# A convolution mixer's products moved to two-bank PSUM form, and VectorE's weight splits put behind short chains at other places

## What is computed

```python
def _swiglu(x, w_gate_up, w_down):
    a, b = jnp.split(x @ w_gate_up, 2, axis=-1)
    return (jax.nn.silu(a) * b) @ w_down

def _short_conv(x, w_in, conv_w, w_out):
    b_gate, c_gate, u = jnp.split(x @ w_in, 3, axis=-1)
    v = c_gate * u
    conv = lax.conv_general_dilated(
        v, conv_w[:, None, :], window_strides=(1,), padding=[(CONV_WIDTH - 1, 0)],
        dimension_numbers=("NWC", "WIO", "NWC"), feature_group_count=D_MODEL)
    return (b_gate * conv) @ w_out
```

## Time and profile before

| | before |
|---|---|
| median of 3 runs | 1669.12 us (1668.87 to 1671.68) |
| the profiled execution, its own time | 1668.95 us |
| span of its trace | 1667.1 us |
| TensorE busy | 1645.2 us (99% of the span) |
| weight loads of TensorE | 1420.7 us (85%) |
| VectorE busy | 1017.7 us (61%) |
| ScalarE busy | 793.6 us (48%) |
| GpSimd busy | 69.0 us (4%) |
| mean granted clock of TensorE | 0.996 |
| moved by DMA | 294.82 MB, mean 177 GB/s |

### The profile page before, as it was taken

The page is one execution under the profiler, slowest core; times in us unless marked ns, Lnnn a source line. Parts: engine busy times, 40 slices in busy tenths (PEclk is TensorE's granted clock), DMA queues, the critical chain, the costliest instruction groups (busy, mean ns, idle before and its releaser), DMA issues.

```text
span 1667.1 us, 22598 instructions
## 1 busy us (share of the span) xinstructions
PE 1645.2 (99%) x9497; PEld 1420.7 (85%) x9497; DVE 1017.7 (61%) x1076; ACT 793.6 (48%) x958; POOL 69.0 (4%) x73
## 2 busy tenths in 40 slices
PE   9999999999999999999999999999999999999999
PEld 7998888889888887888899888888888887688887
DVE  6676655575565557556576556565664477765555
ACT  5334544455454445444543444455443355744443
POOL 0122000000000001000000000000100002000000
PEclk9999999999999999999999999999999999999999
DMA  8534567554356565565565555647545462055562
GB/s 286 163 127 135 189 190 217 200 193 164 125 180 197 177 203 164 200 211 171 189 215 177 173 188 171 209 166 223 196 157 192 171 198 96 1 197 184 176 207 95
DMA packets 221110, 294.82 MB, mean 177 GB/s; under 512 B 7516, under 2 KB 184880, under 8 KB 221010
## 3 DMA queue, kind: packets, MB, share of 16 engines
q1 hardware_dynamic: 215546, 284.40, 51.4%
q10 hardware_dynamic: 5464, 9.00, 2.1%
HBM read 290.75 MB, written 1.57 MB: 175 GB/s over the span
## 4 chain that ended last, share of the span: by engine, by line
PE 86%; DVE 7%; ACT 3%; DMA 2%; issue 1%; POOL 1%; SPq 0%; DVEq 0%; POOLq 0%; ACTq 0%
PE ps L1929 24%; PE ps L2066 18%; PE ps L1931 13%; PE ps L1917 3%; PE ps L1920 3%; PE ps L1918 3%; PE ps L1946 3%; PE ps L1952 3%; PE ps L1947 3%; DVE wlo L1238 2%; PE ps L1996 2%; PE ps L1997 1%; PE ps L1998 1%; PE ps L2182 1%; ACT whi L672 1%
## 5 line engine op out<-in xcount | busy, mean ns | idle before, releaser
L1238 DVE TENSOR_TENSOR wlo<-raw,whi 128x2048 fp32r<-128x2048 f32 (+2 forms) x281 | 603.8, 2166 | 306.8 <-ACT whi L672 305.6
L672 ACT ACTIVATE whi<-raw 128x2048 fp32r<-128x2048 f32 (+1 forms) x265 | 498.4, 1900 | 81.5 <-PE ps L1920 17.9
L1929 PE MATMUL ps<-x_both,whi 128*128 128x512 f32 x1920 | 480.3, 392 | 0.0
L1929 PEld LDWEIGHTS ps<-x_both,whi 128*128 128x128 f32 x1920 | 348.6, 189 | 64.7
L1931 PEld LDWEIGHTS ps<-x_both,wlo 128*128 128x128 f32 x1920 | 261.9, 190 | 18.7
L1931 PE MATMUL ps<-x_both,wlo 128*128 128x256 f32 x1920 | 267.7, 282 | 0.0
L2066 PE MATMUL ps<-whi,hhi 128*128 128x512 f32 x480 | 188.9, 393 | 0.0
L2066 PE MATMUL ps<-wlo,hhi 128*128 128x512 f32 x480 | 188.1, 392 | 0.0
L2066 PE MATMUL ps<-whi,hlo 128*128 128x512 f32 x480 | 187.4, 390 | 0.0
L1917 PE MATMUL ps<-x_both,whi 128*128 128x256 f32 x512 | 127.7, 287 | 0.0
L768 ACT ACTIVATE hid<-ps 128x512 f32<-128x512 f32 x54 | 32.2, 597 | 196.6 <-PE ps L1931 196.5
(11 more groups left out here) (255 smaller groups left out, 1704.6 us busy)
## 6 DMA issues: line engine op xcount, KB each, us to landing
raw<-in_ffn_w_gate_up SPq DMA_DIRECT2D x80, 1024.0 KB, 5.2
raw<-in_ffn_w SPq DMA_DIRECT2D x62, 1024.0 KB, 5.3
raw<-in_ffn_w_down SPq DMA_DIRECT2D x44, 1024.0 KB, 4.8
raw<-in_hgrn_w_in SPq DMA_DIRECT2D x16, 1024.0 KB, 5.5
raw<-in_moba_w_in SPq DMA_DIRECT2D x12, 1024.0 KB, 5.1
raw<-in_conv_w_in SPq DMA_DIRECT2D x10, 1024.0 KB, 5.2
raw<-in_ffn_w_gate_up SPq DMA_DIRECT2D x16, 512.0 KB, 5.0
raw<-in_kv_w SPq DMA_DIRECT2D x6, 1024.0 KB, 5.1
```

The source lines that it names most:

```text
L672: act.activation(whi[s % WRING][:, 0:width], raw[n % RING][:, 0:width], ACT.Copy).then_inc(split_hi, 1)
L1238: ins = dve.tensor_tensor(wlo[s % WRING][:, part], raw[n % RING][:, part], whi[s % WRING][:, part].bitcast(F32), ALU.subtract)
L1929: pe.matmul(ps[:, bank + n, :], hi[:, k, tile], x_both[:, k], start=k == 0, stop=k == KT - 1, skip_group_check=True)
```

## The change

It has four parts.

1. `conv`: `c`, `u` and `b` of all rounds go by `across_pair`, in banks 0-1, 4-5 and 2-3. ScalarE copies the upper part of each (`c_low`, `u_low`, `b_low`), VectorE adds. The first quarter of `cy` is split during round 2 already, into `hhi` and `hlo`. The idle products are gone; the output product begins with the quarter that is ready (`ks=(0, 1)` of both chunks), and goes on with the rest. VectorE's `split(out, 2)` moves behind the last splits of `cy`.
2. `moba`: `scale_probs(3)` stands ahead of `split(out, 2)` on VectorE.
3. Ends of stages: in mixers VectorE's `split(first, 1)` moves behind the two adds of t=0, and ScalarE's squares of t=1 behind `x_high` of t=0. In FFNs the first half of `split(first, 1)` moves behind `normalise` of t=0; in `ffn1` the second half, and the add that follows it, also move behind the second norm's scaling.
4. `ffn4`, rounds 5 to 8: VectorE's `split(d)` moves behind `multiply` and `low_part`.

```diff
@@ scalar: out_product
-                squares(after, 1, 0)
                 x_high(after, 0)
-                squares(after, 1, 1)
+                for half in range(2):
+                    squares(after, 1, half)
                 x_high(after, 1)
@@ scalar: conv
+                def c_low(i):
+                    act.wait_ge(chunk_used, chunks.number[name, "c", i] + 1)
+                    act.wait_ge(gated, i + 1)
+                    act.activation(cgate[:], ps[:, 0:2, S:2 * S], ACT.Copy).then_inc(gate_kept, 1)
+                def u_low(i):
...
+                    act.activation(hid[:], ps[:, 4:6, S:2 * S], ACT.Copy).then_inc(u_low_kept, 1)
+                def b_low(i):
...
+                    act.activation(silu[:], ps[:, 2:4, S:2 * S], ACT.Copy).then_inc(b_low_kept, 1)
...
                 split(name, "u", 1)
+                b_low(0)
                 split(name, "b", 1)
                 for i in range(1, 4):
...
+                    split(*((name, "c", i + 1) if i < 3 else (name, "out", 0)))
+                    c_low(i)
+                    split(*((name, "u", i + 1) if i < 3 else (name, "out", 1)))
+                    u_low(i)
+                    if i == 2:
+                        act.wait_ge(conv_round_done, 1)
+                        act.activation(hhi[:], cy[:, 0:2, :], ACT.Copy).then_inc(yhi_ready, 1)
+                    split(*((name, "b", i + 1) if i < 3 else (name, "out", 2)))
+                    b_low(i)
+                for p in range(1, 4):
@@ vector: out_product
-                for n in range(2):
-                    split(after, "first", n)
+                split(after, "first", 0)
                 for half in range(2):
                     dve.wait_ge(tile_summed, 2 * MIXERS.index(name) + half + 1)
                     add(0, half)
+                split(after, "first", 1)
                 normalise(after, 0)
@@ vector: ffn, in the loop
+                    beside = name == "ffn4" and i in COMPRESS
+                    if beside:
+                        multiply(i)
+                        low_part(i)
                     if i < PAIRS - 2:
                         split(name, "d", i)
                     else:
                         split(name, "u", i + 1)
-                    multiply(i)
-                    low_part(i)
+                    if not beside:
+                        multiply(i)
+                        low_part(i)
@@ vector: ffn, end
                 split(after, "first", 0, parts=(1,))
+                normalise("final" if name == "ffn1" else after, 0)
                 split(after, "first", 1, parts=(0,))
-                normalise("final" if name == "ffn1" else after, 0)
                 add(1, 0)
+                if name == "ffn1":
+                    normalise(after, 0)
                 split(after, "first", 1, parts=(1,))
                 add(1, 1)
                 if name == "ffn1":
-                    normalise(after, 0)
                     normalise("final", 1)
@@ vector: moba
                 moba_max(3)
+                scale_probs(3)
                 split(name, "out", 2)
-                scale_probs(3)
@@ vector: conv, in the loop
+                        split(*((name, "c", i + 1) if i < 3 else (name, "out", 0)))
                         dve.wait_ge(gate_kept, i + 2)
-                        dve.wait_ge(chunk_used, chunks.number[name, "u", i] + 1)
-                        ins = dve.tensor_tensor(cpad[:, :, 2:S + 2], cgate[:], by_two(ps[:, 1, :]), ALU.mult)
-                        ins.then_inc(gated, 1)
+                        link(dve.tensor_tensor(cgate[:], ps[:, 0:2, 0:S], cgate[:], ALU.add))
+                        split(*((name, "u", i + 1) if i < 3 else (name, "out", 1)))
+                        dve.wait_ge(u_low_kept, i)
+                        link(dve.tensor_tensor(hid[:], ps[:, 4:6, 0:S], hid[:], ALU.add))
+                        dve.tensor_tensor(cpad[:, :, 2:S + 2], cgate[:], hid[:], ALU.mult).then_inc(gated, 1)
                         dve.wait_ge(gated, i + 2)
                     taps(i)
+                    if i == 2:
+                        dve.wait_ge(yhi_ready, at.y + 1)
+                        dve.tensor_tensor(hlo[:], cy[:, 0:2, :], hhi[:].bitcast(F32), ALU.subtract).then_inc(ylo_ready, 1)
                     if i < 3:
                         split(name, "b", i + 1)
...
+                    dve.wait_ge(b_low_kept, i + 1)
+                    link(dve.tensor_tensor(silu[:], ps[:, 2:4, 0:S], silu[:], ALU.add))
+                    dve.tensor_tensor(cy[:, 2 * i:2 * i + 2, :], cacc[:], silu[:], ALU.mult).then_inc(conv_round_done, 1)
+                for p in range(1, 4):
...
+                split(name, "out", 2)
                 split(name, "out", 3)
@@ tensor: conv
                 for i in range(1, 4):
-                    pe.wait_ge(gate_kept, i + 1)
-                    if i == 1:
-                        pe.wait_ge(gated, 2)
-                    across(0, name, "c", i)
                     pe.wait_ge(gated, i + 1)
-                    across(1, name, "u", i)
+                    across_pair(0, name, "c", i)
+                    across_pair(4, name, "u", i)
                     pe.wait_ge(conv_round_done, i)
-                    across(2, name, "b", i)
-                keep_warm(6)
-                out_product(name)
+                    across_pair(2, name, "b", i)
+                pe.wait_ge(gated, 5)
+                out_first(name, 0, first=(hhi, hlo), ks=(0, 1))
+                pe.wait_ge(conv_round_done, 4)
+                out_first(name, 1, first=(hhi, hlo), ks=(0, 1))
+                for n in range(2):
+                    out_first(name, n, first=(hhi, hlo), ks=(2, 3))
+                out_last(name, first=(hhi, hlo))
```

36 lines of the change are left out of this document (9 added, 27 removed).

## The result

| | us |
|---|---|
| before, median of 4 runs | 1669.74 (1668.87 to 1671.68) |
| changed, median of 4 runs | 1658.93 (1654.65 to 1659.44) |
| ratio | 0.993, 95% interval 0.9913 to 0.9947 |
| forecast | 1650.7 (1646 to 1658) |
| profiled execution of the change | 1659.44, span 1657.6 (before: 1668.95, span 1667.1) |

Faster, as forecast, but by 10.8 us (9.5 between the two profiled executions) in place of 18.3, and just outside the range.

The account below looks back on a forecast made before the run. TensorE, busy 1645.2 of 1667.1 us, was taken as the bound, with waits and the slow stretches behind them as the loss. Terms 1.8 + 5.1 + 4.2 + 6.4 + 2.0 + 0.8 - 2.0 = 18.3 us gave 1650.7, range 1646 to 1658.

Parts of the forecast that it names:

- Part 1, `conv` (6.9): `conv`: fewer matmuls per half give 1.8 us; removing the idle products' seam and its slow matmuls gives 5.1.
- slack of 0.5 us ahead of the second piece: `conv`, output product: first piece's 12 matmuls take 2.7 us, the hand-overs TensorE then waits for 2.2: 0.5 to spare.
- cover of the added copies and adds: `conv`'s rounds: extra copy and add per chunk cost 0, since 3 us of cover remains before TensorE needs `gated`.
- slower rival: `conv`: `gated` comes late and TensorE stops ahead of `c` in three rounds, 23 us, 1673.5 in all; chance 0.04.
- Part 2, `moba` (4.2): `moba`, transposes of the probabilities: 2.6 us wait goes, with a slow stretch of 1.6; gain 4.2 us.
- Part 4, `ffn4` (6.4): `ffn4`, rounds 5 to 7: waits for `hlo` ahead of `compress` and the slow stretch vanish; gain 6.4 us.
- the ring: `ffn4`: `compress`, split, `d`'s 7.74 us transfer, its split, copy, `hlo` chain: 20.2 us against TensorE's 20.3, hardly any slack.
- first rival: `ffn4`: `d`'s transfer lands 1 us later, rounds 6 and 7 wait again; gives back 2 to 6.4 us; chance 0.16.
- Part 3, FFN ends (0.8): Ends of `ffn0`, `ffn2`, `ffn3`, `ffn4`: t=0 wait goes, t=1 transposes wait 0.4; net gain 0.2 each, 0.8 us.
- Part 3, mixers (2.0) and `ffn1` (-2.0): Mixer ends: waits removed, root held 1.1 to 1.4 us, gain 2.0; `ffn1`'s end: late add delays first product, loss 2.0.
- Third rival, the lock: Mixer ends: root held by the split's whole 2.3 us, transposes 1 us later, two slow stretches: 7 us, 1658; chance 0.08.
- fourth rival: More gain than reckoned: `ffn1`'s wait leaves the clock high (+1.6), small end-of-stage waits not seen (+2): 1647; chance 0.10.

Follow-up runs that it names:

- undo_conv: Changed kernel with all of part 1 undone (`conv` of the kernel before on all three engines): 1658.53 us, ratio 0.9929.
- undo_moba: Changed kernel with `scale_probs(3)` behind `split(out, 2)` again on VectorE: 1660.77 us, ratio 0.9946.
- only_ffn4: Kernel before with part 4 alone (VectorE's split of `d` moved in `ffn4`'s rounds): 1662.61 us, ratio 0.9957.
- shift78: Changed kernel with 78 more TensorE instructions (156 waits that hold already) ahead of the first product: 1653.68 us, ratio 0.9899.
- again: Changed kernel run and profiled once more, nothing edited: 1657.99 us, ratio 0.9924.
- undo_ffn1: Changed kernel with VectorE's order at `ffn1`'s end as in the kernel before: 1654.87 us, ratio 0.991.
- both: Changed kernel, ScalarE's copy and high part ahead of its split of `d` in `ffn4`, both t=1 adds earlier at `ffn1`'s end: 1650.85 us, ratio 0.9882.

## Why the prediction was right or wrong

- **Part 1, `conv` (6.9).** Right: 6.9 in the stage (6.7 in the table, less 0.2 at its end), 7.0 in undo_conv. The slack of 0.5 us ahead of the second piece was there (0.4), the rounds wait for nothing, and the cover of the added copies and adds held, so the slower rival never came near. What failed is the silent assumption that an edit costs or gains only where it stands. Leaving out 167 matmuls moved the instruction packets in a stage over 300 us later.
- **Part 2, `moba` (4.2).** Right: 4.3 in undo_moba.
- **Part 4, `ffn4` (6.4).** This step failed, at "the ring". As worked out it was right: 210.6 to 210.9 us in only_ffn4 and shift78, a gain of 6.6 and 6.7. But it took the 7.74 us of the earlier trace rows as the transfer's price in the changed kernel. There it was 8.5 to 9.2, and most of that became waits: 0.8 and 1.0 us by starts in rounds 6 and 7, and behind the second a slow stretch of twice the usual length that cost 3.3. That is the **first rival**, word for word ("if the transfer of `d` lands only 1 us later"), given 0.16. Its price of 2 to 6.4 holds 4.9; the time it gave, 1653 to 1657, is missed by the rest of this list. What I weighed against it, the round "sped up in its own waits", was no argument against a later transfer. The slack itself was larger than the 0.1 reckoned: in the changed kernel, in again, undo_ffn1 and undo_moba the first `d` took 0.7 to 1.3 us longer than in shift78, and the wait in round 6 was 0.2 to 0.8, each time 0.5 less.
- **Part 3, FFN ends (0.8).** Mis-sized: 0.1. The 0.4 us ahead of t=0 and some 0.3 between its halves went as forecast, but at t=1 0.64 is lost by starts, not 0.4: net 0.03, four times.
- **Part 3, mixers (2.0) and `ffn1` (-2.0).** Right: 1.8 over the four mixers (0.3, 1.3, -0.2 and 0.4 in their order; `conv`'s and `moba`'s are inside their lines in the table), whose terms as written add up to 1.9, and -2.2 with the forecast chain of add, square and `x_high`, link by link. The slow stretch that the term half expected came in six profiles of seven.
- **Third rival, the lock.** The roots of the mixers were held by 1.1 us, as in the sum, not for a whole split: at `conv`'s end GpSimd's step of 1.44 us began 1.0 us into a split of 2.28 and ended 0.2 behind it. The Trainium skill (SBUF — State Buffer, "Who interferes with whom") has the instruction issued first win. The trace agrees in the mixers, but not at the FFNs' ends, though the prediction says so: there the step of the earlier trace rows began at 833.88, the second half split at 833.98, and the step was held to the end of that one; in the run both it began 0.3 us ahead of the split and was held as well. By the recorded starts the step was first each time; why the split still won is not shown.
- **What was not forecast at all.** The first weights' landing moved by chance by up to 2.5 us, and slow stretches at unchanged places: 2.8 us between the two profiles. The prediction had named "slow stretches at places other than `ffn1`'s end" as what would prove it wrong. Its range rested on rivals in the change and allowed nothing for this (its lower end of 1646 is 1 us under the fourth rival's 1647, from no row). The runs of one kernel show its size: those of the kernel before span 4 to 7 us in each group of experiments, and the changed kernel's first four are 1654.65 with a granted clock of 1.000 and 1658.65 to 1659.44 with 0.996. So that the median came out above 1658 is in part bad luck; that 4.9 us of `ffn4` are missing is not.

## What to carry to other kernels

A wait that hangs on a transfer with no slack is not removed by shaving the chain behind it: take the work off that chain altogether (here by ScalarE's copy ahead of its split), or count the term as won only if the transfer may come a microsecond later. And before an edit changes the number of TensorE's instructions, ask which tight transfers come later in the kernel. Compare two profiles by stages before explaining any part: a stage that the edit doesn't touch and that still moved is the finding.

## What the runs showed of the hardware

- TensorE's instructions come by DMA, 16 KB for each 256, and one such packet (some 1.1 us on one DMA engine, in two cases 2.2) goes with a delay of about as much of a 1 MB transfer that it meets: 7.5 to 8.0 us became 8.1 to 9.6, and 5.1 became 6.9 and 7.0.
- Waits that hold already cost TensorE time: 78 added instructions of two waits each put the first transposes off by 3.3 us, 100 by 5.5, 178 by 13.9. Why it grows faster than their number is open.
- GpSimd's first step of the root took 0.3 us alone and up to 1.7 beside VectorE's splits, and at the FFNs' ends and in the run both it was held to the end of a split that began 0.1 to 0.3 us behind it.
- The same wait of 2.2 to 2.6 us left the granted clock high in 4 of 17 cases. In the changed kernel a wait of 1.0 us ahead of `compress` was followed by a stretch at 1.2 GHz that cost 3.3 us, while one of 1.15 us in the kernel before (round 6) was not. The length of the wait alone doesn't decide, and I did not find what does.
